# Dilated and banded attention: a step's transposes issued before its value products

## The chip, the cores and the metric

The program runs on one core of a Trainium2 chip, in one launch. Its time is the device time in microseconds, as the median of several executions. A core has five engines with a queue of instructions each: TensorE (PE, whose weight loads stand in the profile as PEld), VectorE (DVE), ScalarE (ACT), GpSimd (POOL) and SyncE (SP, which here only issues DMAs). They wait for each other by semaphores.

## The reference

Two layers of an encoder on 1024 tokens of width 1024, in float32. In each layer one input projection feeds four branches of attention: A (latent attention) and B (grouped queries) see all tokens; C is dilated, with 12 heads in three groups of dilation 1, 4 and 16 and 64 steps to either side; D is banded, 4 heads with 128 tokens to either side and a learned sink. Each branch is gated, projected and merged. What matters here is the banded core of C and D, in the reference's words:

```python
logits = jnp.einsum("bnqkgd,bnskd->bnkgqs", qb, kband).astype(jnp.float32) * scale + bias
logits = jnp.where(mask[None, :, None, None], logits, NEG_INF)
m = jnp.max(logits, axis=-1, keepdims=True)
...
    e = jnp.exp(logits - m)
    ssum = jnp.sum(e, axis=-1, keepdims=True)
p = (e / ssum).astype(v.dtype)
out = jnp.einsum("bnkgqs,bnskd->bnqkgd", p, vband).reshape(b, lp, hk, g, dv)[:, :L]
```

## The kernel before

The attention is cut into units: one head and 128 queries, against 128 to 384 keys. A layer has 32 units in A, 32 in B, 96 in C (six passes of 16 units, two for each dilation) and 32 in D. The order on every engine is written out by hand as one loop over steps, and a unit passes through several steps.

On TensorE, for C (`n == 2`) and D (`n == 3`), step `s` does the following, in this order:

- the logits of unit `s` (L1119 and L1120: two products 256 or 384 columns wide), after a wait for the maxima of unit `s-2`;
- the value products of unit `s-3` (`values`, L1145): the transposed probabilities from `ptsb`, as the stationary operand, times 64 columns of values, one product for each chunk of 128 keys. They wait until VectorE has copied the unit's transposes out of PSUM (L2130), and until the output bank is free;
- the transposes of the probabilities of unit `s-2` (`transposes`, L1130), one for each chunk, into one of two PSUM banks. They wait for the exponentials (ACT, L1530) and for the bank;
- in C, in the first two or three steps of each pass, transposes of values (`value_transposes`, L982), which wait for ScalarE's copy of the projected values (L1563);
- filler work: in C ten 512-wide products of the next pass's projection (L961; eight in the last pass; the 15th step of a pass has four and the 16th none, in the passes that have 144 products to place), in D fifteen 512-wide products of the merge of branch C (also L961). A filler that begins a PSUM bank waits until VectorE has emptied it (L1983).

Each product in plain float32 stands in the trace as two records with a weight load each: a unit of C with two chunks has four L1145 records, one with three chunks six. A transpose has one.

On VectorE a step has the biased minimum of unit `s` (L1882), in D the outputs of unit `s-3` (L1933), the copy of the transposes of unit `s-2` to `ptsb` (L2130), and now and then the rests of the next pass's operands (L1983). On ScalarE it has the exponential of unit `s` (L1530), in C the copy of the output of unit `s-3` (L1537) with a store, and the emptying of filler banks (L1563, L1569).

The numbers of the PSUM banks and the counts on the semaphores follow from a plan made ahead (`plan_units`), in the order of the transposes alone.

Of the kernel before, what the change touches and what calls it, by code (L numbers as in the profile page):

```python
# [129 lines left out]
def build(nc, x, norm_g, w_in, q_norm_g, kv_norm_g, w_q_up, w_kv_up, gqa_q_g, gqa_k_g, win_sink,  # L130
          t5_table, w_branch, w_out, final_g, c_onehot, c_mask, c_rope_a, c_rope_b, c_ident,
          out):
    with ExitStack() as ctx:
# [257 lines left out]
        def wait_tbank(eng, g, l):  # L391

            if g >= 2:
                who, n = tgroups[g - 2]
                eng.wait_ge((t_freed_dve if who == "dve" else t_freed_act)[l], n)
# [32 lines left out]
        for n in range(NB):  # L428
# [13 lines left out]
            if n == 0:  # L442
                t = []
                u0 = len(units)
# [6 lines left out]
            elif n == 1:  # L451
                t = []
                u0 = len(units)
# [7 lines left out]
            elif n == 2:  # L461
                for g, r in enumerate(STRIDES):
                    L = S // r
                    table_g = bias_mid if g == 1 else biasb
                    for hp in range(2):
                        t = [tile([(C_OFF + w * C_W + g * BW + hp * P, P, 0)]) for w in (1, 0, 2)]
                        u0 = len(units)
# [30 lines left out]
            else:  # L498
# [5 lines left out]
                u0 = len(units)  # L504
# [25 lines left out]
        def lags(u0):  # L530

            return (1, 2, 3) if units[u0]["ring"] == 2 else (2, 3, 4)
# [163 lines left out]
        def freed(l, f):  # L696

            signal, count = fill_freed_at[f]
            return signal[l], count
# [10 lines left out]
        def inc(ins, signal, n=1):  # L710

            ins.then_inc(signal, n)
# [198 lines left out]
        def _(pe):  # L911
# [5 lines left out]
            for l in range(DEPTH):  # L917
# [45 lines left out]
                def fills_part(f0, tt, m0, m1):  # L963

                    for m in range(m0, min(m1, 2 * len(tt) * FILL_MMS)):
                        j, i = divmod(m, FILL_MMS)
                        t, f = tt[j // 2], f0 + j
                        if i == 0:
                            pe.wait_ge(w_split[l], t + 1)
                            wait_fill(f)  # L970
                        ins = one_product(ps[:, fill_bank[f], :], t, j % 2, i)
                        if i == FILL_MMS - 1:
                            inc(ins, fill_ready[l])

                def value_transposes(p, v):
                    g, idx, rows = p["v_groups"][v]
                    if v == 0:

                        pe.wait_ge(*freed(l, p["fill"] + (5 if "g" in p else 7)))
                    wait_tbank(pe, g, l)  # L980
                    for i, wi in enumerate(idx):
                        ins = pe.transpose(ps[0:rows, 4 + g % 2, i * P:(i + 1) * P],  # L982
                                           window_tokens(p["windows"][wi], STRIDES[p["g"]] if "g" in p else 1),
                                           ident[:, :])
                    inc(ins, t_ready[l])

                def wait_operands(p):

                    if "g" not in p:
                        pe.wait_ge(t_freed_act[l], tgroups[p["v_groups"][-1][0]][1])  # L990
                    pe.wait_ge(*freed(l, p["fill"] + (3 if "g" in p else 5)))
                    pe.wait_ge(stack_twice[l], 4 * fill_copy[p["fill"] + 1][2])
                    if p is branches[2]["passes"][0]:
                        pe.wait_ge(*freed(l, p["fill"] + 5))
# [116 lines left out]
                def logits(s):  # L1111
                    u = units[s]
                    q_rest = u.get("q_rest")
                    if q_rest is not None:
                        pe.wait_ge(aq_set[l], s // 2 + 1)
                    for c in range(0, u["k"].shape[1], HALF):
                        w = min(HALF, u["k"].shape[1] - c)
                        dst = u["product_at"][:, c:c + w]
                        pe.matmul(dst, u["q"], u["k"][:, c:c + w], start=True, stop=False)  # L1119
                        ins = pe.matmul(dst, u["q"], u["k_rest"][:, c:c + w], start=False, stop=q_rest is None)  # L1120
                        if q_rest is not None:
                            ins = pe.matmul(dst, q_rest, u["k"][:, c:c + w], start=False, stop=True)  # L1122
                    inc(ins, lg_ready[l])

                def transposes(s):
                    pe.wait_ge(exp_done[l], s + 1)
                    for g, chunks in units[s]["groups"]:
                        wait_tbank(pe, g, l)
                        for i, (m, c0, _) in enumerate(chunks):
                            ins = pe.transpose(ps[0:m, 4 + g % 2, i * P:(i + 1) * P],  # L1130
                                               units[s]["prob"][:, c0:c0 + m], ident[:, :])
                        inc(ins, t_ready[l])

                def values(s, u0):
                    nonlocal pg
                    u = units[s]
                    if s - 2 >= u0:
                        v = units[s - 2]
                        pe.wait_ge(o_freed_dve[l] if v["who"] == "dve" else o_freed_act[l], v["o_count"])
                    n, total = 0, len(u["chunks"])  # L1140
                    for g, chunks in u["groups"]:
                        who, count = tgroups[g]
                        pe.wait_ge(t_freed_dve[l] if who == "dve" else t_freed_act[l], count)
                        for i, (m, _, v) in enumerate(chunks):
                            ins = pe.matmul(u["o"], ptsb[0:m, pg % 2, i * P:(i + 1) * P], v,  # L1145
                                            start=n == 0, stop=n == total - 1)
                            n += 1
                        pg += 1
                    inc(ins, pv_done[l])
# [83 lines left out]
                for b in branches:  # L1233
                    n = b["n"]
                    p = b["passes"][0]
                    u0, u1 = b["span"]
# [97 lines left out]
                    lt, lv, ly = lags(u0)  # L1334
                    keys_tile = branches[3]["passes"][0]["tiles"][:1]
                    if n >= 2:
                        for s in range(u0, u1 + ly):
                            k, i = divmod(s - u0, 16)
                            if s < u1:
                                if n == 2 and k and i == 0:  # L1340
                                    wait_operands(b["passes"][k])
                                if s - 2 >= u0:

                                    pe.wait_ge(nm_set[l], s - 1)
                                logits(s)
                            if n == 3 and s - lv == u0:
                                pe.wait_ge(*freed(l, b["gate_fill"] + 3))
                            if u0 <= s - lv < u1:
                                if n == 2 and (s - lv - u0) % 16 == 0:
                                    pe.wait_ge(t_freed_act[l], tgroups[b["passes"][(s - lv - u0) // 16]["v_groups"][-1][0]][1])  # L1350
                                values(s - lv, u0)
                            if u0 <= s - lt < u1:
                                transposes(s - lt)
                            if n == 2 and s < u1:
                                if i < len(b["passes"][k]["v_groups"]):
                                    value_transposes(b["passes"][k], i)
                                if k + 1 < len(b["passes"]):

                                    after = b["passes"][k + 1]
                                    fills_part(after["fill"], after["tiles"], PART * i, PART * (i + 1))  # L1360
                                else:
                                    fills_part(b["gate_fill"], b["gate_tiles"] + keys_tile, GATE_PART * i, GATE_PART * (i + 1))
                            if n == 2 and s >= u1:
                                m = GATE_PART * 16 + TAIL_PART * (s - u1)
                                fills_part(b["gate_fill"], b["gate_tiles"] + keys_tile, m, m + TAIL_PART)
                            if n == 3 and s < u1:
                                merge_part(15 * (s - u0), 15 * (s - u0 + 1))
                            if n == 3 and 0 <= s - u1 < 2:

                                pe.wait_ge(nm_set[l], u1)  # L1370
                                merge_gate_ahead(b, s - u1)
                            if n != 2 and u0 <= s - ly < u1 and units[s - ly]["head"] == HEADS - 1:
                                v = units[s - ly]
                                pe.wait_ge(o_freed_dve[l], v["o_count"])
                                y_transposes(next(y), yn[:, v["st"] % 2, :])
                        for v in units[u1 - 2:u1]:
                            pe.wait_ge(o_freed_dve[l] if v["who"] == "dve" else o_freed_act[l], v["o_count"])
# [1108 lines left out]
```

## Time and profile before

| what | value |
| --- | --- |
| median of 3 runs | 2727.71 us (2723.93 to 2729.89) |
| the profiled execution | 2725.23 us, its span 2723.4 us |
| TensorE busy | 2643.5 us, 97% of the span |
| weight loads busy | 2216.6 us, 81% |
| VectorE, ScalarE, GpSimd busy | 1286.8, 1039.8, 897.5 us |
| chain that ended last | PE 87%, DVE 5%, ACT 4% |

The profile is one execution. A line of it names the source line, the engine, the operation and the operands. A TensorE record's start is when the product was let in, and its end is modelled, so that neighbouring records overlap: lengths are best read from the start of one product to the start of a later one of the same kind. The stretches with C are 683 to 965 us and 2024 to 2305 us, those with D 1025 to 1180 us and 2365 to 2520 us.

### The profile page before, as it was taken

How to read it: one execution, taken by the hardware profiler on the slowest of the kernel's cores; microseconds unless marked ns; L12 is line 12 of the kernel's file. 1: busy time of each engine (PE TensorE's matmuls, PEld its weight loads, DVE VectorE, ACT ScalarE, POOL GpSimd, SP SyncE). 2: the span in 40 equal slices, each digit the busy share in tenths (PEclk: the TensorE clock that was granted, in tenths of full speed). 3: DMA queues.
4: the chain of work that ended last, by engine and by line, in shares of the span. 5: the costliest groups of instructions: out<-in, count | busy, mean ns of one | idle time of the engine just before them, and what ended most of it. 6: DMA issues, size and time to landing. Idle time of an engine off the chain costs nothing.

```text
span 2723.4 us, 36386 instructions
## 1 busy us (share of the span) xinstructions
PE 2643.5 (97%) x13796; PEld 2216.6 (81%) x13796; DVE 1286.8 (47%) x2697; ACT 1039.8 (38%) x2138; POOL 897.5 (33%) x634
## 2 busy tenths in 40 slices
PE   7999999999999999999999999999999999999998
PEld 5688878878888888878897878888888888888787
DVE  3575365722344365542346734575224343555223
ACT  4385115611444525521225831175024445354111
POOL 2274331033243342233423734200334342422232
PEclk9999999999999999999999999999999999999999
DMA  4200111021111231111420011100211113211122
GB/s 145 63 9 19 50 44 30 1 55 47 41 48 49 61 95 44 30 39 45 157 75 9 9 38 49 45 10 1 70 40 51 47 44 94 65 39 30 49 101 93
DMA packets 201415, 138.02 MB, mean 51 GB/s; under 512 B 20968, under 2 KB 187496, under 8 KB 201208
## 3 DMA queue, kind: packets, MB, share of 16 engines
q1 hardware_dynamic: 187420, 129.21, 16.7%
q10 hardware_dynamic: 13824, 6.49, 0.8%
q8 instruction: 112, 1.84, 0.3%
q14 instruction: 59, 0.48, 0.1%
HBM read 120.77 MB, written 19.10 MB: 51 GB/s over the span
## 4 chain that ended last, share of the span: by engine, by line
PE 87%; DVE 5%; ACT 4%; issue 2%; DMA 1%; SPq 1%; POOL 1%; ACTq 0%; POOLq 0%; DVEq 0%
PE ps L961 24%; PE ps L924 10%; PE ps L926 10%; PE ps L925 10%; PE ps L1199 5%; PE ps L1145 4%; PE ps L1164 3%; PE ps L1027 3%; PE ps L1029 3%; PE ps L1028 3%; PE ps L1119 3%; PE ps L1120 2%; PE ps L1130 2%; ACT prob L1530 1%; PE ps L1440 1%
## 5 line engine op out<-in xcount | busy, mean ns | idle before, releaser
L2356 POOL CAST wh<-wraw 128x1024 fp32r<-128x1024 f32 (+3 forms) x148 | 167.3, 1131 | 1551.1 <-PE ps L926 788.3
L924 PE MATMUL ps<-xh,wh 128*128 128x512 f32 x1088 | 426.7, 392 | 2.2 <-ACT pt_split L1756 2.2
L926 PE MATMUL ps<-xh,wl 128*128 128x512 f32 x1088 | 423.7, 389 | 0.0
L925 PE MATMUL ps<-xl,wh 128*128 128x512 f32 x1088 | 423.4, 389 | 0.0
L2358 POOL TENSOR_TENSOR wl<-wraw,wh 128x1024 fp32r<-128x1024 f32 (+3 forms) x148 | 391.5, 2646 | 11.9
L961 PE MATMUL ps<-xh,wh 128*128 128x512 f32 x896 | 366.4, 409 | 5.2 <-POOL wl L2358 2.5
L961 PE MATMUL ps<-xh,wl 128*128 128x512 f32 x896 | 357.3, 399 | 0.0
L961 PE MATMUL ps<-xl,wh 128*128 128x512 f32 x896 | 356.4, 398 | 0.0
L1585 ACT ACTIVATE gs<-ps 128x512 f32<-128x512 f32 x96 | 57.0, 598 | 518.5 <-PE ps L926 514.0
L924 PEld LDWEIGHTS ps<-xh,wh 128*128 128x128 f32 x1088 | 204.3, 188 | 44.2 <-ACT pt_split L1756 3.0
L926 PEld LDWEIGHTS ps<-xh,wl 128*128 128x128 f32 x1088 | 204.2, 188 | 43.0
L925 PEld LDWEIGHTS ps<-xl,wh 128*128 128x128 f32 x1088 | 204.4, 188 | 41.6
L2085 DVE TENSOR_TENSOR pt_slots<-ps,pt_slots 128x512 fp32r<-128x512 f32 x256 | 171.5, 685 | 83.4 <-ACT pt_slots L1674 81.6
L961 PEld LDWEIGHTS ps<-xh,wh 128*128 128x128 f32 x896 | 168.9, 188 | 39.4 <-issue 9.5
L961 PEld LDWEIGHTS ps<-xh,wl 128*128 128x128 f32 x896 | 168.6, 188 | 33.7
L961 PEld LDWEIGHTS ps<-xl,wh 128*128 128x128 f32 x896 | 169.2, 189 | 30.2 <-issue 1.0
L1530 ACT ACTIVATE prob<-prob,cst 128x192 f32<-128x192 f32 (+2 forms) x192 | 86.7, 451 | 270.3 <-DVE cst L1882 270.2
L1882 DVE CUSTOM_DVE_ANT_0 prob<-ps,biasb 128x256 f32<-128x256 f32 (+3 forms) x192 | 77.3, 402 | 224.6 <-PE ps L1120 223.4
L2004 DVE TENSOR_TENSOR gs<-ps,gs 128x512 f32<-128x512 f32 x64 | 44.2, 690 | 269.9 <-ACT gs L1585 266.6
L1674 ACT ACTIVATE pt_slots<-ps 128x512 fp32r<-128x512 f32 x256 | 148.5, 600 | 31.9 <-PE ps L1164 26.0
L1874 DVE TENSOR_REDUCE nm<-ps 128x1 f32<-128x1024 f32 x128 | 155.6, 1216 | 8.9 <-PE ps L1122 6.3
L1164 PE MATMUL ps<-ident,prob 128*128 128x128 f32 x864 | 129.2, 277 | 11.4 <-DVE pt_slots L2085 4.8
(308 smaller groups left out, 5216.7 us busy)
## 6 DMA issues: line engine op xcount, KB each, us to landing
wraw<-in_w_in_dram SPq DMA_DIRECT2D x128, 512.0 KB, 3.9
acc<-in_x_dram SPq DMA_DIRECT2D x16, 512.0 KB, 6.8
wraw<-in_w_branch_dram SPq DMA_DIRECT2D x64, 128.0 KB, 3.9
wraw<-in_w_out_dram SPq DMA_DIRECT2D x16, 512.0 KB, 3.5
dil_out<-cst ACTq DMA_DIRECT2D x96, 66.0 KB, 1.6
toep<-toep_row SPq DMA_DIRECT2D x16, 256.0 KB
xres<-acc SPq DMA_DIRECT2D x8, 512.0 KB, 2.6
acc<-xres SPq DMA_DIRECT2D x8, 512.0 KB, 7.4
```

Of the source, the lines that this page charges most:

```text
L924: pe.matmul(dst, ah, bh, start=i == 0, stop=False)
L925: pe.matmul(dst, ah, bl, start=False, stop=False)
L926: last = pe.matmul(dst, al, bh, start=False, stop=i == len(ks) - 1)
L961: return pe.matmul(dst, w, x_part, start=m == 0, stop=m == 3 * len(ks) - 1)
L1164: ins = pe.transpose(ps[0:m, 4 + g % 2, i * P:(i + 1) * P], units[s]["prob"][:, c0:c0 + m], ident[:, :])
L1199: ins = pe.matmul(u["product"], v, pair_probs((s - 3 - later) // 2, rest, j), start=j == 0 and rest == 0, stop=j == ST - 1 and rest == 1)
L1530: inc(act.activation(dst, src, ACT.Exp, bias=bias, scale=-1.0, accum_out=total), exp_done[l])
L1674: inc(act.activation(pt_slots[:, x % SLOTS, 0, 4 * part:4 * part + 4, :], ps[:, 4 + g % 2, :].rearrange("p (j t) -> p j t", t=P), ACT.Copy ...
L1874: inc(dve.tensor_reduce(dst, u["logits"], AX.X, ALU.min), nm_set[l])
L2085: inc(dve.tensor_tensor(pt_slots[:, slot, 1, some, :], ps[:, 4 + g % 2, :].rearrange("p (j t) -> p j t", t=P), pt_slots[:, slot, 0, some, ...
L2356: inc(pool.tensor_copy(high, raw), w_hi[l])
L2358: ins = pool.tensor_tensor(rest, raw, high.bitcast(F32), ALU.subtract)
```

## The change

In the step loop of TensorE for C and D, the value products of unit `s-3` are remembered and issued behind the transposes of unit `s-2`. The wait for the value groups of a pass (`t_freed_act`) stays where it was, ahead of both.

```diff
@@ -1348,9 +1348,13 @@
                             if u0 <= s - lv < u1:
                                 if n == 2 and (s - lv - u0) % 16 == 0:
                                     pe.wait_ge(t_freed_act[l], tgroups[b["passes"][(s - lv - u0) // 16]["v_groups"][-1][0]][1])
-                                values(s - lv, u0)
+                                ready_values = s - lv
+                            else:
+                                ready_values = None
                             if u0 <= s - lt < u1:
                                 transposes(s - lt)
+                            if ready_values is not None:
+                                values(ready_values, u0)
                             if n == 2 and s < u1:
                                 if i < len(b["passes"][k]["v_groups"]):
                                     value_transposes(b["passes"][k], i)
```

An ordinary step of C on TensorE, before (in these rows x2 counts instructions, not records; `yh` holds queries, `att_split` keys):

```order
L961 MATMUL ps<-xh,wl 128x512
L1119 MATMUL ps<-att_split,yh 128x256
L1120 MATMUL ps<-att_split,yh 128x256
L1145 MATMUL ps<-rows_buf,ptsb 128x64 x2
L1130 MATMUL ps<-ident,prob 128x128 x2
L961 MATMUL ps<-xh,wh 128x512
```

and now:

```order
L961 MATMUL ps<-xh,wl 128x512
L1119 MATMUL ps<-att_split,yh 128x256
L1120 MATMUL ps<-att_split,yh 128x256
L1130 MATMUL ps<-ident,prob 128x128 x2
L1145 MATMUL ps<-rows_buf,ptsb 128x64 x2
L961 MATMUL ps<-xh,wh 128x512
```

The value products now stand directly in front of a 512-wide product; before, a transpose stood between.

The last step of a pass of C and the first of the next on TensorE, before:

```order
L1119 MATMUL ps<-att_split,yh 128x256
L1120 MATMUL ps<-att_split,yh 128x256
L1145 MATMUL ps<-rows_buf,ptsb 128x64 x2
L1130 MATMUL ps<-ident,prob 128x128 x2
L1119 MATMUL ps<-bk_stack,yl 128x256
L1120 MATMUL ps<-bk_stack,yl 128x256
L1145 MATMUL ps<-rows_buf,ptsb 128x64 x2
L1130 MATMUL ps<-ident,prob 128x128 x2
L982 MATMUL ps<-ident,prob 128x128 x4
L961 MATMUL ps<-xh,wh 128x512
```

and now:

```order
L1119 MATMUL ps<-att_split,yh 128x256
L1120 MATMUL ps<-att_split,yh 128x256
L1130 MATMUL ps<-ident,prob 128x128 x2
L1145 MATMUL ps<-rows_buf,ptsb 128x64 x2
L1119 MATMUL ps<-bk_stack,yl 128x256
L1120 MATMUL ps<-bk_stack,yl 128x256
L1130 MATMUL ps<-ident,prob 128x128 x2
L1145 MATMUL ps<-rows_buf,ptsb 128x64 x2
L982 MATMUL ps<-ident,prob 128x128 x4
L961 MATMUL ps<-xh,wh 128x512
```

Here the value products of the first step still have a transpose behind them (L982), and those of the last step now a 256-wide product. In D the same exchange is made with three chunks:

```order
L1120 MATMUL ps<-bk_stack,att_split 128x384
L1130 MATMUL ps<-ident,prob 128x128 x3
L1145 MATMUL ps<-rows_buf,ptsb 128x64 x3
L961 MATMUL ps<-xh,wh 128x512
L961 MATMUL ps<-xl,wh 128x512
```

Counted over the whole order of now, 232 groups of L1145 have a product that is no transpose behind them (218 an L961, 10 an L1119, 4 an L924); before, 2 had. The other engines run the same instructions in the same order as before.

## Rows read from the trace of the kernel before

**Rows 1.** Busy time in the two stretches of C and of D.

```profile
core 0: us, PE busy (x) PEld busy (x) DVE busy (x) ACT busy (x) POOL busy (x), PEclk, DMA share, GB/s
683.00:965.00 282.00, 278.66 (x1585) 238.94 (x1586) 113.01 (x344) 132.31 (x366) 101.88 (x76) 1.00 0.20 51
1025.00:1180.00 155.00, 154.68 (x839) 133.18 (x838) 88.56 (x259) 79.93 (x147) 37.88 (x18) 1.00 0.13 35
```

**Rows 2.** TensorE's waits in the first C, 683 to 965 us.

```profile
PE ps L1145 <- DVE ptsb L2130: 2.1, 5, 0.4
PE ps L961 <- DVE yl L1983: 0.6, 1, 0.6
PE ps L982 <- ACT prob L1563: 0.2, 1, 0.2
```

**Rows 3.** Timeline of TensorE: an ordinary step of C.

```profile
692.55 0.28 PE L1120 MATMUL ps<-att_split,yh 128*128 128x256 f32 x1
692.67 0.56 PE L1145 MATMUL ps<-rows_buf,ptsb 128*128 128x64 f32 x4
693.06 0.39 PE L1130 MATMUL ps<-ident,prob 128*128 128x128 f32 x2
693.21 0.48 PE L961 MATMUL ps<-xh,wh 128*128 128x512 f32 x1
693.52 0.40 PE L961 MATMUL ps<-xl,wh 128*128 128x512 f32 x1
```

**Rows 4.** Timeline of TensorE: end of C, value products with and without a transpose behind.

```profile
962.83 0.39 PE L961 MATMUL ps<-xh,wl 128*128 128x512 f32 x1
963.06 0.33 PE L1145 MATMUL ps<-att,ptsb 128*128 128x64 f32 x2
963.22 0.28 PE L1130 MATMUL ps<-ident,prob 128*128 128x128 f32 x1
963.26 0.48 PE L961 MATMUL ps<-xh,wh 128*128 128x512 f32 x1
963.57 0.40 PE L961 MATMUL ps<-xl,wh 128*128 128x512 f32 x1
...
964.04 0.39 PE L961 MATMUL ps<-xh,wh 128*128 128x512 f32 x1
964.27 0.33 PE L1145 MATMUL ps<-att,ptsb 128*128 128x64 f32 x2
964.40 0.48 PE L961 MATMUL ps<-xl,wh 128*128 128x512 f32 x1
964.72 0.40 PE L961 MATMUL ps<-xh,wl 128*128 128x512 f32 x1
```

**Rows 5.** Timeline of TensorE in A: four 64-wide records behind two transposes.

```profile
540.00 0.38 PE L1219 MATMUL ps<-ident,rows_buf 128*128 128x128 f32 x2
540.21 0.56 PE L1187 MATMUL ps<-fold,ptsb 128*128 128x64 f32 x4
540.61 0.61 PE L1164 MATMUL ps<-ident,prob 128*128 128x128 f32 x4
```

**Rows 6.** Timeline of TensorE in A: four 64-wide records ahead of 512-wide products.

```profile
553.92 0.55 PE L1187 MATMUL ps<-fold,ptsb 128*128 128x64 f32 x4
554.28 0.48 PE L924 MATMUL ps<-xh,wh 128*128 128x512 f32 x1
554.60 0.39 PE L925 MATMUL ps<-xl,wh 128*128 128x512 f32 x1
554.83 0.40 PE L926 MATMUL ps<-xh,wl 128*128 128x512 f32 x1
```

**Rows 7.** Timeline of TensorE, last and first step of two passes of C.

```profile
729.25 0.28 PE L1120 MATMUL ps<-att_split,yh 128*128 128x256 f32 x1
729.36 0.55 PE L1145 MATMUL ps<-rows_buf,ptsb 128*128 128x64 f32 x4
729.75 0.39 PE L1130 MATMUL ps<-ident,prob 128*128 128x128 f32 x2
...
730.10 0.28 PE L1120 MATMUL ps<-bk_stack,yl 128*128 128x256 f32 x1
730.82 0.63 PE L1145 MATMUL ps<-rows_buf,ptsb 128*128 128x64 f32 x4 [0.44 <-DVE ptsb L2130]
731.28 0.39 PE L1130 MATMUL ps<-ident,prob 128*128 128x128 f32 x2
731.51 0.60 PE L982 MATMUL ps<-ident,prob 128*128 128x128 f32 x4
```

**Rows 8.** Timeline of VectorE in the same steps.

```profile
729.64 0.29 DVE L1882 CUSTOM_DVE_ANT_0 prob<-ps,biasb 128x192 f32<-128x192 f32 x1
730.25 0.42 DVE L2130 COPY ptsb<-ps 128x256 f32<-128x256 f32 x1 [0.31 <-PE ps L1130]
```

**Rows 9.** Timeline of ScalarE in the same steps.

```profile
728.19 0.46 ACT L1530 ACTIVATE prob<-prob,cst 128x192 f32<-128x192 f32 x1 [2.40 <-DVE cst L1882]
728.55 0.19 ACT L1530 ACTIVATION_READ_ACCUMULATOR prob<-prob,cst 128x1 f32 x1
730.53 0.58 ACT L1563 ACTIVATE prob<-ps 128x512 f32<-128x512 f32 x1
```

**Rows 10.** Timeline of TensorE: a filler product that waits for its bank.

```profile
762.38 0.40 PE L961 MATMUL ps<-xh,wl 128*128 128x512 f32 x1
762.83 0.47 PE L961 MATMUL ps<-xh,wh 128*128 128x512 f32 x1
```

## The prediction

> **What bounds the kernel now.** I read the busy time by stretch first, then TensorE's waits, then the timeline of single steps. In the stretches of C and D TensorE is busy for 278.66 of 282 us and 154.68 of 155 us, at full granted clock (1.00), and no other engine is over half busy there [rows 1] but for VectorE and ScalarE in D, at 57% and 52%. So the reader is to see that in these loops nothing is late except TensorE itself: every nanosecond that its order costs is added to the span, and the most that a better cover of waits can bring is what TensorE waits. That is 2.1 us for the copy of the transposes, in 5 waits of a layer [rows 2], 4 us in both layers.
>
> **What the change takes away.** The value products wait for the copy (L2130) only where the filler work is missing, at the turn of a pass: L1145 starts at 730.82, 0.15 behind the end of the copy at 730.67, where TensorE could have had it at 730.10 + 0.12 = 730.22 [rows 7, 8]. With the transposes first, both ends of this wait move. The copied transposes are issued 0.39 earlier in the step before (at 729.36 and not 729.75 [rows 7]); the copy then follows the minimum that ends at 729.93 and ends near 730.40 [rows 8]. The value products come behind two transposes, at 730.22 + 0.22 = 730.44, and wait until 730.40 + 0.15 = 730.55. The wait is nearly gone. What is late next is the transposes of values, L982: they need ScalarE's L1563, which ends at 731.11 [rows 9], and with the same 0.15 they cannot start before 731.26. They start at 731.51 now [rows 7]. So a turn gains 0.25 us, not 0.6. There are five turns in a layer; at the fifth L982 already waits for L1563 [rows 2], and there the gain is nothing. The term is 8 x 0.24 = 1.9 us.
>
> **What it adds.** No instruction is added, but the neighbours change. Read how long a group of 64-wide records takes by what stands behind it. Behind a product comes the group, then a transpose: four records take 693.06 - 692.67 = 0.39 [rows 3] and 540.61 - 540.21 = 0.40 [rows 5], two take 0.16 [rows 4]. With a 512-wide product behind, the start of that product is recorded early (0.03 behind a transpose, and the product after it 0.31 later, where two 512-wide ones stand 0.23 apart), so I read to the second one: four records take 554.60 - 553.92 - 0.23 = 0.45 [rows 6]. For two records, from a 512-wide product to the second one behind the group: 964.72 - 964.04 = 0.68 without a transpose, 963.57 - 962.83 = 0.74 with one [rows 4]. A transpose takes 0.11 (0.21 for two in rows 5), so it should have added 0.11 and adds 0.06. Both readings say the same: a 64-wide record that has a transpose behind it is 0.05 us shorter than one with anything else behind it, each other one being 0.11. The transposes themselves cost the same with either neighbour: two of them ahead of a 64-wide record take 0.21 [rows 5].
>
> Before, every group of value products had a transpose behind it, in all but 2 cases. Now 232 have an L961, L1119 or L924, which makes 230 more (84 steps in each C, the 95 with both parts less the 11 in which L982 follows; 31 steps in each D). An ordinary step goes from 0.97 (692.55 to 693.52 [rows 3]) to 1.02. Start times are rounded to 0.01, so the price lies between 0.04 and 0.06; I take 0.047, and 230 x 0.047 = 10.8 us. The bounds are 230 x 0.06 = 13.8 above, and nothing below, if 512-wide weights can be got ready behind a 64-wide record in this place, which no row shows.
>
> The Trainium skill (TensorE: Matmul & The Clock Gate, LDWEIGHTS) gives a load as P/1.2, by which an estimate for 128 columns is 107 ns, and its section "Step-by-step: what each phase is for" says that TensorE pulls the next load ahead of running products. By the second rule alone the order would be free and the sum would be the gain of 1.9 us; the records against it are those of rows 4 and 6, and the first rule fits the 0.11 of each record.
>
> **What of it is hidden.** In four of the six passes of a layer (the second to the fifth) one filler waits for its bank: it comes at 762.83 and not at 762.61 [rows 10], and after an idle 0.6 in the fifth pass [rows 2]. That wait ends by a chain through ScalarE and VectorE which starts at the logits of the step before, and two groups of value products lie between. It is at least 0.2 long, so it swallows 2 x 0.047 each time: I count 8 of them, 0.8 us. The last step of a pass ends in the wait for L1563, which swallows its 0.047 ten times: 0.5 us.
>
> **Costed at nothing.** The transposes are issued 0.39 earlier (0.61 in D) relative to their exponentials; at 731.28 the exponential of that unit had ended at 728.74 [rows 7, 9], and a step takes over 1.7 us even where it has no filler. The bank that they wait for was read by a copy one step before. The value products end 0.2 to 0.3 later in the step; ScalarE's copy of the output stands behind an exponential that ends later still, and in D VectorE has idle time. SP, POOL and the DMAs see no change.
>
> **The sum.** 10.8 - 1.9 - 0.8 - 0.5 = +7.6 us. Against the profiled execution's own 2725.2 us that is 2732.8; it lies 2.5 us below the median of the runs, so against the median of 2727.7 I forecast 2735.3, rounded to 2735 us, slower by 0.28%.
>
> **The rivals.**
>
> 1. Faster: the load is hidden after all. Then the wait at the turns is all that changes. For it speaks the wait that is there; against it that the price was read in two places of different width and agrees. Its time is 2727.7 - 1.9 = 2725.8, down to 2723.6 if L982 had not to wait and the whole 4.1 us went. It decides at the first L961 behind the value products: with a pitch of 0.97 for the step and not 1.02 it is this one. Chance 0.13.
> 2. Partly paid: the price is as read, but the waits swallow more of it, since a slower TensorE meets banks that are already free, or some groups pay less than those of rows 4 and 6. With 120 to 150 of the 230 groups paying, 5.6 to 7 less 3.2: 2730 to 2732, within 0.2%. Against it: outside the turns and 8 bank waits no wait stands in these stretches [rows 1, 2]. Chance 0.14.
> 3. Slower than that: a price also between transposes and 64-wide records, which rows 5 show to be absent at one place only, or 0.06 and not 0.047, with no gain at the turns: 13.8 to 16, so 2741 to 2744. Chance 0.07.
> 4. The change does nothing, because the transposes wait for exponentials in every step and the order is made good: nearly excluded, since the exponential has 2.5 us in hand at a turn, where steps are shortest [rows 7, 9]. 2728, chance 0.02.
>
> **How the numbers follow.** The forecast has 0.64, with its own range 2731 to 2739: the price from 0.04 to 0.06 gives +5.9 to +10.5, and the median moves by 1 or 2 us on its own. For 8 in 10 I add rival 2 and part of rival 1: 2726 to 2740. What a measurement of this kernel can tell from no change is 0.2%, 5.5 us: slower begins at 2733.2. The forecast's own range lies mostly above it (0.54 of its 0.64), rival 3 wholly: slower 0.61. Same: 0.10 of the forecast, rivals 2 and 4 and most of rival 1: 0.34. Faster: 0.05.
>
> **What would show it.** In the changed kernel an ordinary step of C should go from L1120 to the second L961 in 1.02 us instead of 0.97, and its whole pitch from 3.17 to 3.22; a step of D should grow by 0.05 as well. The idle time of L1145 for L2130 should fall from 4.1 us to under 1, and L982 should wait for L1563 at every turn. The stretches of C should grow by about 2.7 us each and those of D by 1.5 each; wider groups of value products should not cost more than narrow ones. The prediction is wrong if the step keeps its 0.97, or if the stretches grow while the step does not.

## The result, and the profile after

Against the kernel before, run on the same chips, the changed one takes 2732.25 us in the median of 15 runs (2730.29 to 2736.33) where the one before takes 2725.44 us: a ratio of 1.0025, 95% interval 1.0018 to 1.0032. It is 6.8 us slower, a quarter of a per cent, and the interval does not reach 1. The forecast was 7.6 us slower, 2735 us, with its own range from 2731 to 2739. The profiled execution of the changed kernel has a span of 2730.2 us, also 6.8 more than before.

The busy times of the same two stretches, which now begin and end a little later (columns as in [rows 1]):

```profile
683.00:968.00 285.00, 282.82 (x1587) 243.51 (x1588) 107.53 (x344) 132.93 (x367) 102.36 (x76) 1.00 0.19 50
1028.00:1184.00 156.00, 155.68 (x837) 133.43 (x836) 88.58 (x259) 79.92 (x147) 37.85 (x18) 1.00 0.13 35
```

TensorE is as full as it was, and the same number of products takes longer. VectorE is busy 5.5 us less in C with as many instructions, because its copies of the transposes now find their data and overlap the end of the minimum ahead of them; the idle time in front of the copies of two chunks was 17.0 us in C before and is 0.3:

```profile
L2134 DVE COPY ptsb<-ps 128x256 f32<-128x256 f32 x64 | 27.0, 422 | 0.3 <-PE ps L1145 0.3
```

That is a great deal of waiting taken from an engine that is not the bottleneck, and it is worth nothing but the turns. The ordinary step of C on TensorE's timeline, the one of [rows 3], and the start of the next step:

```profile
692.86 0.28 PE L1119 MATMUL ps<-att_split,yh 128*128 128x256 f32 x1
692.97 0.28 PE L1120 MATMUL ps<-att_split,yh 128*128 128x256 f32 x1
693.09 0.38 PE L1130 MATMUL ps<-ident,prob 128*128 128x128 f32 x2
693.31 0.56 PE L1145 MATMUL ps<-rows_buf,ptsb 128*128 128x64 f32 x4
693.68 0.48 PE L961 MATMUL ps<-xh,wh 128*128 128x512 f32 x1
693.99 0.40 PE L961 MATMUL ps<-xl,wh 128*128 128x512 f32 x1
...
696.07 0.28 PE L1119 MATMUL ps<-gs_split,yh 128*128 128x256 f32 x1
```

From L1120 to the second L961 it is 693.99 - 692.97 = 1.02 us, where [rows 3] have 0.97. The pitch, from the L1119 of one step to the L1119 of the next, is 3.21 us (696.07 - 692.86). The four value records and the first filler take 0.68 (693.31 to 693.99), less 0.23 for the filler: 0.45, as the four of [rows 6].

The turn of a pass, which answers to [rows 7], with ScalarE's copy of the values ([rows 9]):

```profile
730.15 0.28 PE L1120 MATMUL ps<-att_split,yh 128*128 128x256 f32 x1
730.27 0.38 PE L1130 MATMUL ps<-ident,prob 128*128 128x128 f32 x2
730.49 0.56 PE L1145 MATMUL ps<-rows_buf,ptsb 128*128 128x64 f32 x4
...
731.06 0.28 PE L1120 MATMUL ps<-bk_stack,yl 128*128 128x256 f32 x1
731.17 0.38 PE L1130 MATMUL ps<-ident,prob 128*128 128x128 f32 x2
731.39 0.57 PE L1145 MATMUL ps<-rows_buf,ptsb 128*128 128x64 f32 x4
732.08 0.66 PE L982 MATMUL ps<-ident,prob 128*128 128x128 f32 x4
```

```profile
731.44 0.59 ACT L1567 ACTIVATE prob<-ps 128x512 f32<-128x512 f32 x1
```

The value products no longer wait for the copy of the transposes. L982 does wait: it starts at 732.08, right behind the end of ScalarE's L1567 at 732.03. From the L1120 of the last step to L982 it is 1.93 us, where [rows 7] have 2.26. TensorE's waits in C say the same, against [rows 2]: L1145 has gone from the list, and L982 has 0.4 instead of 0.2. That one wait of L982 is at the fifth turn. At the other four the list names none, since the modelled ends of the value products reach over the idle time; there the starts show it, with 1.92 or 1.93 us from the L1120 of the last step to L982 at each of the eight turns of both layers. The 0.8 us of L1119 is no news: it stands ahead of the first logits of C, and the kernel before has it too, though [rows 2] do not list it (the row by itself, which is of before).

```profile
PE ps L1119 <- ACT prob L1567: 0.8, 1, 0.8
PE ps L961 <- DVE yl L1987: 0.5, 1, 0.5
PE ps L982 <- ACT prob L1567: 0.4, 1, 0.4
```

```profile
PE ps L1119 <- ACT prob L1563: 0.8, 1, 0.8
```

To compare the stretches of all kernels I take the start of the first and the last logits of a stretch (L1119; C begins with `gs_split` and ends with `bk_stack`, D is `bk_stack,att_split`). For the changed kernel, where the columns after the count are the duration in ns (least, median, most) and the first and last start:

```profile
L1119 PE MATMUL ps<-bk_stack,yl x48: 277/278/366, 730.9 to 961.9; 128*128 128x256 f32 x48
L1119 PE MATMUL ps<-gs_split,yh x24: 277/278/366, 683.7 to 921.8; 128*128 128x256 f32 x24
L1119 PE MATMUL ps<-bk_stack,att_split x32: 277/333/421, 1028.5 to 1173.7; 128*128 128x384 f32 x24, 128*128 128x256 f32 x8
```

The last column is the median distance from one L1119 to the next, over the steps of C with two chunks and ten fillers.

| kernel (profiled execution) | first C, us | first D, us | ordinary step of C, us |
| --- | --- | --- | --- |
| before | 276.2 | 144.0 | 3.17 |
| changed | 278.2 | 145.2 | 3.21 |
| transposes on both sides (e1) | 275.4 | 144.0 | 3.17 |
| new order at the turns alone (e2) | 275.1 | 144.0 | 3.17 |
| one by one in turn (e5) | 272.6 | 141.8 | 3.11 |
| the same, transpose first at the turns (e6) | 272.1 | 141.8 | 3.11 |
| order before, 128 columns of values (e3) | 279.3 | 145.3 | 3.20 |
| order now, 128 columns of values (e4) | 278.4 | 145.1 | 3.21 |
| order before, plain products for transposes (e7, one run) | 296.2 | 154.3 | 3.44 |

The changed kernel's growth sits in these stretches: 2.0 and 2.2 us in the two C, 1.3 in each D (from the unrounded starts), 6.8 in all. What lies outside them differs by less than 0.1 us in sum, though parts of it differ by up to 1.0 (see the last section).

### The profile page after: what moved, and what is told of

It reads as the page before. It is cut to its first block, busy times and chain, and to the rows that moved or that the text cites. A ratio compares the mean times of both kernels' runs of the same rounds, so it can differ in the third digit from the quotient of the medians.

```text
span 2730.2 us, 36382 instructions
## 1 busy us (share of the span) xinstructions
PE 2652.1 (97%) x13796; PEld 2225.1 (81%) x13796; DVE 1276.0 (47%) x2697; ACT 1039.6 (38%) x2138; POOL 897.0 (33%) x634
## 4 chain that ended last, share of the span: by engine, by line
PE 87%; DVE 5%; ACT 4%; issue 2%; DMA 1%; SPq 1%; POOL 1%; ACTq 0%; POOLq 0%; DVEq 0%
PE ps L961 24%; PE ps L924 10%; PE ps L926 10%; PE ps L925 10%; PE ps L1199 5%; PE ps L1145 3%; PE ps L1164 3%; PE ps L1027 3%; PE ps L1029 3%; PE ps L1028 3%; PE ps L1119 3%; PE ps L1120 2%; PE ps L1130 2%; ACT prob L1534 1%; PE ps L1444 1%
## 5 line engine op out<-in xcount | busy, mean ns | idle before, releaser
L924 PE MATMUL ps<-xh,wh 128*128 128x512 f32 x1088 | 426.6, 392 | 2.2 <-ACT pt_split L1760 2.2
L961 PE MATMUL ps<-xh,wh 128*128 128x512 f32 x896 | 366.1, 409 | 5.2 <-POOL wl L2362 2.7
L961 PE MATMUL ps<-xh,wl 128*128 128x512 f32 x896 | 357.1, 399 | 0.0
L961 PE MATMUL ps<-xl,wh 128*128 128x512 f32 x896 | 356.5, 398 | 0.0
L924 PEld LDWEIGHTS ps<-xh,wh 128*128 128x128 f32 x1088 | 204.3, 188 | 44.4 <-ACT pt_split L1760 3.0
L961 PEld LDWEIGHTS ps<-xh,wh 128*128 128x128 f32 x896 | 169.0, 189 | 39.3 <-issue 9.4
L961 PEld LDWEIGHTS ps<-xh,wl 128*128 128x128 f32 x896 | 168.7, 188 | 33.4
L961 PEld LDWEIGHTS ps<-xl,wh 128*128 128x128 f32 x896 | 169.1, 189 | 30.3 <-issue 1.0
```

The source lines that it names most:

```text
L924: pe.matmul(dst, ah, bh, start=i == 0, stop=False)
L961: return pe.matmul(dst, w, x_part, start=m == 0, stop=m == 3 * len(ks) - 1)
```

## The experiments

**e1: the value products between the transposes.** In the step, all transposes but the last go ahead, the last one behind.

```diff
-                                values(s - lv, u0)
-                            if u0 <= s - lt < u1:
-                                transposes(s - lt)
+                                both = u0 <= s - lt < u1
+                                if both:
+                                    mixed(s - lv, s - lt, u0, lambda nv, nt: "t" * (nt - 1) + "v" * nv + "t")
+                                else:
+                                    values(s - lv, u0)
+                            elif u0 <= s - lt < u1:
+                                transposes(s - lt)
```

`mixed` issues the same products with the same waits, in the order of the letters. On record before it ran:

> The value products stand between the transposes: all transposes of the step but the last ahead of them, the last one behind. Theory N (what costs is the neighbour behind the last value product: 0.05 us whenever it is no transpose): an ordinary step of C keeps the pitch of before, 3.17 us, the stretches of C and D keep their 280.9 and 161.0 us, and the time is that of before to within 2 us. Rival F (the step pays because transposes now stand directly behind the logits, or because value products stand behind a transpose): the pitch is 3.21 as in the changed kernel and the time is 5 to 7 us over before.

Measured: ratio to before 0.9989 (0.9980 to 0.9997); C 275.4, D 144.0. A step on TensorE's timeline:

```profile
700.79 0.28 PE L1120 MATMUL ps<-gs_split,yh 128*128 128x256 f32 x1
700.91 0.28 PE L1177 MATMUL ps<-ident,prob 128*128 128x128 f32 x1
701.02 0.56 PE L1167 MATMUL ps<-rows_buf,ptsb 128*128 128x64 f32 x4
701.41 0.28 PE L1177 MATMUL ps<-ident,prob 128*128 128x128 f32 x1
701.45 0.48 PE L961 MATMUL ps<-xh,wh 128*128 128x512 f32 x1
701.76 0.40 PE L961 MATMUL ps<-xl,wh 128*128 128x512 f32 x1
```

A transpose stands directly behind the logits and value products directly behind a transpose, as in the changed kernel, and yet L1120 to the second L961 is 0.97, and the pitch stays at 3.17. D is as before to 0.1 us. (The 280.9 and 161.0 us of the expectation are from another way to count a stretch than the table's; what was to be tested is that the stretches keep their length.) Rival F falls; what counts is what stands behind the last value product. The time came out 3 us under before, where I had allowed 2: each C is 0.8 shorter, since at the turns the value products come behind a transpose and wait 1.3 us in all and not 2.1; the rest of the 3 us is outside C and D, where the edit changes nothing.

**e2: the new order at the turns alone.**

```diff
+                                turn = n == 2 and s < u1 and (k and i == 0 or i == 15 and k + 1 < len(b["passes"]))
+                                if turn:
+                                    transposes(s - lt)
                                 values(s - lv, u0)
-                            if u0 <= s - lt < u1:
+                            else:
+                                turn = False
+                            if u0 <= s - lt < u1 and not turn:
```

> The new order only in the last step of a pass of C and in the first step of the next one (10 turns, so 20 steps of 254); everywhere else the order of before. Theory N with the turn as I worked it out: 10 groups pay 0.047, which falls into a wait, and 8 turns gain 0.25 us: 2 us under before, too little for the comparison, but the stretches of C shrink by 1.0 us each and those of D not at all. Rival W (a wait saved at a turn is given back within the pass, by the next wait for a bank): stretches of C as before to within 0.3 us.

Measured: 0.9993 (0.9984 to 1.0002), not to be told from no change; C 275.1, so 1.1 shorter, and D 144.0, the same. The gain at the turns shows in the stretches, not in the medians. It is kept to the end of the stretch and has the size of the forecast, 1.0 us. Rival W falls.

**e5: value products and transposes one by one in turn.** The order is `"".join("v" * (i < nv) + "t" * (i < nt) for i in range(4))` in the call above.

> Value products and transposes one by one in turn: value, transpose, value, transpose. Counted over the order, 488 of 496 value products have a transpose behind them, where before 254 had one and in the changed kernel 24. Theory N: 234 more short ones than before, 0.047 each: 11 us under before, 0.4%; an ordinary step of C has a pitch of 3.13 instead of 3.17, a step of D is 0.09 shorter. Rival L (the last record of the whole group is short only because the load of the transposes starts while several products of one bank are in flight, so it is one saving a step): no change from before. Rival F (each change between the two kinds costs): slower than before by 234 x 2 x 0.02, some 10 us.

Measured: 0.9961 (0.9949 to 0.9974), 11 us under before. A step:

```profile
701.73 0.28 PE L1120 MATMUL ps<-att_split,yh 128*128 128x256 f32 x1
701.85 0.33 PE L1167 MATMUL ps<-rows_buf,ptsb 128*128 128x64 f32 x2
702.02 0.28 PE L1177 MATMUL ps<-ident,prob 128*128 128x128 f32 x1
702.14 0.33 PE L1167 MATMUL ps<-rows_buf,ptsb 128*128 128x64 f32 x2
702.31 0.28 PE L1177 MATMUL ps<-ident,prob 128*128 128x128 f32 x1
702.34 0.48 PE L961 MATMUL ps<-xh,wl 128*128 128x512 f32 x1
702.66 0.39 PE L961 MATMUL ps<-xh,wh 128*128 128x512 f32 x1
```

Now both value products of the unit have a transpose behind them, and L1120 to the second L961 is 0.93. The saving comes once for each pair of a value product and a transpose behind it, so it is no matter of the group. It is 11 us for 234 more such pairs, 0.047 each. That is a mean: the pitch in C fell by 0.06 to 3.11 where 3.13 was expected, of which 0.05 is between L1120 and the second L961 (0.973 to 0.924 in the median) and the rest among the fillers, and D fell by 2.2 us, which is 0.04 for each of its pairs. Why the two differ stays open. Rivals L and F fall.

**e6: as e5, with the transpose first in each pair at the turns** (the condition of e2).

> The last one with the transpose first in the last step of a pass of C and the first step of the next. Theory N with the turn: 1 to 2 us under the kernel that alternates everywhere, all of it in the stretches of C (some 0.2 us a turn, in four turns of five). Rival W: the same as that kernel.

Measured: 0.9952 (0.9940 to 0.9965), 2710.91 us in the median on a chip where before takes 2725.78. C is 0.5 shorter than in e5 and D the same, so some 1 us for both layers, the lower end of what was expected. This version beats both kernels: by 0.5% the one before, and so, by the two ratios, by some 0.7% the changed one, which it was not run against.

**e3 and e4: value products of 128 columns, in the order of before and of now.** Each takes the values of two heads; half of the result is not used. The edit shown is that of the dilated units with two chunks; those with one chunk and the units of D are widened in the same way, and the product writes `u["wide"]`.

```diff
-                                    chunks = [(P, x, cv[hp][:, place[(c, first + x)], cols]) for x in (0, P)]
+                                    chunks = [(P, x, cv[hp][:, place[(c, first + x)], :]) for x in (0, P)]
...
-            u["o"] = ps[:, 6 + s % 2, 0:HD]
+            u["wide"] = ps[:, 6 + s % 2, 0:2 * HD]
+            mine = more["e"] if "e" in more else more["head"] // 2
+            u["o"] = ps[:, 6 + s % 2, mine * HD:(mine + 1) * HD]
```

> The order of before, but each value product of C and D takes 128 columns of values (those of two heads, of which one is used) instead of 64, so its pass through the array takes as long as a transpose's. Theory E (a 64-wide record is done in about 0.06 us and then stands waiting for the next weights, which take 0.11; in front of a transpose they are there sooner): with 128 columns each record fills its 0.11, the saving in front of a transpose is gone, and doubling the values costs just that: 254 x 0.047 = 12 us less what waits swallow, so the stretches of C grow by 2.2 to 3 us each, those of D by 1.4, as in the changed kernel, and the step of C has a pitch of 3.21. Rival M (a change of mode: whatever stands in front of a transpose is cheap): records stay 0.05 short in front of a transpose, C and D as before, 3.17. Rival R (the width counts in full, as for 512-wide ones): each of the 992 records costs 0.05 more, 45 us in all.

> The changed kernel's order with the same 128 columns of values. Theory E: nothing but the 24 products that still have a transpose behind them can grow: the time of the changed kernel plus at most 1 us, a pitch of 3.21 in C, and the same time as the wide kernel in the order of before to within the gain at the turns (2 us). Rival M: as the changed kernel too, but then 10 us over the wide kernel in the order of before. Rival R: 45 us over the changed kernel.

Measured: e3 1.0036 (1.0022 to 1.0051), e4 1.0032 (1.0019 to 1.0045). The step of e3, in the order of before:

```profile
701.31 0.28 PE L1122 MATMUL ps<-gs_split,yh 128*128 128x256 f32 x1
701.43 0.61 PE L1147 MATMUL ps<-rows_buf,ptsb 128*128 128x128 f32 x4
701.88 0.38 PE L1132 MATMUL ps<-ident,prob 128*128 128x128 f32 x2
702.01 0.48 PE L963 MATMUL ps<-xh,wh 128*128 128x512 f32 x1
702.33 0.39 PE L963 MATMUL ps<-xl,wh 128*128 128x512 f32 x1
```

Four records ahead of a transpose take 0.45 where the 64-wide ones took 0.39 [rows 3], L1120 to the second L963 is 1.02, and the pitch is 3.20. D is as long as in the changed kernel, C longer by about the gain at the turns that only the new order has; its 3.1 us over before are a little more than the 2.2 to 3 expected. In the changed kernel's order the doubled width costs nothing in the stretches: C 278.4 against 278.2, D 145.1 against 145.2. (The ratio of e4 is 0.0007, 1.9 us, above that of the changed kernel; the two intervals overlap, and the stretches show none of it.) Rivals M and R fall. It fits theory E, that of a 64-wide record's 0.11 about half is idle unless a transpose stands behind it; the idle half itself no row shows.

**e7: plain products with the identity in place of the transposes,** in the order of before.

```diff
-                            ins = pe.transpose(ps[0:m, 4 + g % 2, i * P:(i + 1) * P],
-                                               units[s]["prob"][:, c0:c0 + m], ident[:, :])
+                            ins = pe.matmul(ps[0:m, 4 + g % 2, i * P:(i + 1) * P],
+                                            units[s]["prob"][:, c0:c0 + m], ident[:, :], start=True, stop=True)
```

> The order of before, with the transposes of probabilities in C and D made by plain float32 products with the identity instead of transposes, so each has two records. One look at the step. If the short last record belongs to a transpose behind it, the value products are now 0.05 longer (0.44 to 0.45 for four records in front of them, and a step of C of 3.17 + 0.22 + 0.05 = 3.44 us). If it belongs to any float32 product with the identity as moving operand, or to 128 columns behind 64, they stay 0.39 and the step is 3.39.

Measured (one run, 2788.52 us):

```profile
712.22 0.28 PE L1119 MATMUL ps<-gs_split,yh 128*128 128x256 f32 x1
712.34 0.28 PE L1120 MATMUL ps<-gs_split,yh 128*128 128x256 f32 x1
712.46 0.56 PE L1145 MATMUL ps<-rows_buf,ptsb 128*128 128x64 f32 x4
712.85 0.66 PE L1130 MATMUL ps<-ident,prob 128*128 128x128 f32 x4
715.66 0.28 PE L1119 MATMUL ps<-att_split,yh 128*128 128x256 f32 x1
```

The two readings that I put together came apart. The pitch is 3.44, which says that the saving has gone: two more records at 0.11 make 0.22, and there is 0.05 on top. But the value group still takes 0.39 from its start to the next group's start, where 0.44 to 0.45 was expected. The 0.05 stands in the group behind. I go by the pitch, since the loop pays that: the saving belongs to a transpose behind the value product, not to the identity or to 128 columns. By the pitch alone the 0.05 could also be a cost of the plain products themselves; the weight loads under "The cause" speak against that. It also shows that a distance of starts between two kinds of record is not their cost.

## Why the prediction was right

**The price.** The step was forecast to go from 0.97 to 1.02 and did; D's step with three chunks was to grow by 0.05, and D grew by 1.3 us over 144 (1.29 unrounded), which is 31 steps of 0.042. The pitch in C came to 3.21, not 3.22; the fillers behind the group make up for a little of the price. So the mechanism was right and the price over the whole loop was 0.042, at the low end of the 0.04 to 0.06 that the prediction gave: 9.7 us for 230 groups, not 10.8. e5 has 0.047 in the mean, with the opposite sign. The price was read from starts of different kinds of record [rows 3, 5]; e7 shows that this reading can mislead. What held it up were the readings from one 512-wide product to another [rows 4].

**The turn.** A gain of 0.25 was forecast. From the last step's L1120 to L982 the time fell by 0.33, but the first L982 record is then longer; to the first filler behind, by 0.28. At the other turns that was 0.23 to 0.25, and at the fifth nothing, as said: 2.0 us in all, where the sum has 1.9. The successor wait was named rightly: L982 for ScalarE's copy. The value products were to keep a wait of 0.11 there and have none, since the copy starts before the minimum ahead of it has ended and is done 1.03 us behind the L1120 of the last step, where the prediction had 1.15; as L982 ends the turn, that slip cost the forecast nothing.

**What is swallowed.** The wait for a bank answers to [rows 10] in these rows of the changed kernel:

```profile
763.26 0.40 PE L961 MATMUL ps<-xh,wl 128*128 128x512 f32 x1
763.67 0.47 PE L961 MATMUL ps<-xh,wh 128*128 128x512 f32 x1
```

It is 0.41 instead of 0.45. So it swallowed 0.04 and not the 0.09 of the forecast. The other three of the first C swallowed 0.08, 0.05 and 0.07; in the second C two swallowed 0.03 and 0.07, one nothing, and one wait grew by 0.04. That makes 0.3 us where the sum has 0.8. The prediction treated each such wait as one that takes in all of a delay, and they took in less than half.

**The sum.** It gave +7.6, of which 2.3 in each C and 1.5 in each D. The stretches from the first logits to the last grew by 2.0 and 2.2 us and by 1.3 each. With the terms as measured it is 9.7 - 2.0 - 0.3 - 0.5 = 6.9 (the last term not measured by itself), against the 6.8 of the stretches. Two slips partly cancel: the price was 1.1 us too high and what is swallowed 0.5 too high; that the total came so near owes something to luck. Of the 3 us between 2735 and the measured 2732.25, 2.3 are the median of before, taken from three runs. In its last part the prediction put the growth of C at 2.7, which does not follow from its own sum; the sum was right and that figure was not.

**The rivals.** That the load is hidden (1) is excluded by the step and, with a cause, by e3 and e4. That only part of the groups pays (2) is excluded by the pitch of every common kind of step: in C 3.17 became 3.21, 2.37 became 2.42, 2.82 became 2.88 and 1.79 became 1.83; in D 4.87 became 4.92, and 4.75 and 4.73 became 4.78. That transposes cost something ahead of value products (3) is excluded by e1. That the exponentials hold up the transposes (4) did not happen: no L1130 stands among the waits.

**The cause.** Shown: a value product of 64 columns is shorter by 0.05 when a transpose stands behind it (e1, e5), and not when it is itself 128 columns wide (e3); e7 says the same of a plain product of the same operands in the transpose's place, by its pitch. That fits a load of 0.11 us for the next weights which a record of 0.06 cannot cover, and a load for a transpose which takes about half of that.

The trace has the weight loads as records of their own (PEld), and they bear this out. These are the loads of the transposes in the first C (ns: least, median, most) in the changed kernel, e5 and e7, and last the value products' in the changed kernel:

```profile
L1130 PEld LDWEIGHTS ps<-ident,prob x160: 137/142/144, 689.9 to 965.3; 128*128 128x128 f32 x160
L1177 PEld LDWEIGHTS ps<-ident,prob x158: 192/194/200, 695.7 to 962.6; 128*128 128x128 f32 x158
L1130 PEld LDWEIGHTS ps<-ident,prob x302: 188/192/192, 691.8 to 964.7; 128*128 128x128 f32 x151
L1145 PEld LDWEIGHTS ps<-rows_buf,ptsb x160: 186/192/193, 693.2 to 930.7; 128*128 128x128 f32 x160
```

Where there is nothing to save (now, and in e3 with a median of 141), the load of a transpose is recorded with 142 ns and that of a plain product with 192, so 0.05 less; with plain products in their place (e7) the 192 is back. In e5, where every transpose stands behind a 64-wide value product, its load is recorded with 194: it starts some 0.06 us behind the load before it, where the loads of plain products start 0.11 apart, so it begins the saved 0.05 sooner. As far as the recorded ends can be trusted, the loads of transposes are shorter by the size of the price. What remains argued is that the load alone makes the saving: no run changes the length of a load and nothing else. The Trainium skill (TensorE: Matmul & The Clock Gate, LDWEIGHTS) has loads at P/1.2, an estimate of 107 ns for 128 columns. That agrees with the 0.11 at which plain records follow each other, but not with the 192 ns that such a load is recorded with, nor with what stands in front of a transpose.

## What to carry to other kernels

Where TensorE is full, the order of its products has a price of its own. Here a product of 64 columns did not cover the load of the weights behind it: a transpose behind it saved 0.05 us, and widening it to 128 columns was free where no transpose followed. When an edit swaps two groups, look at all the neighbours that change, find each pair somewhere else in the trace, and multiply by the count: a gain of 0.25 us at 8 turns was outweighed by some 0.04 us at 230 steps. Read prices from one record to the next of the same kind, around the whole group.

## What the runs showed that I had not expected

The alternating order, which only turned the finding round, is worth 11 us, and 15 with the turns (12.5 of them in the stretches of C and D), more than the change under study.

Part of the spread between executions lies outside C and D, and the traces show two sources of it. One is the granted clock. Two neighbouring stretches of the second layer in the kernel before (columns as in [rows 1]):

```profile
1772.00:1775.30 3.30, 1.66 (x7) 0.71 (x5) 2.91 (x3) 2.68 (x4) 3.22 (x2) 1.00 0.00 0
1775.30:1778.70 3.40, 3.36 (x12) 2.87 (x13) 1.32 (x3) 1.69 (x3) 0.64 (x1) 0.50 0.48 109
```

In the second of them the clock lay at the lower of its two levels (1.2 and 2.4 GHz); in the first, still at the upper one, TensorE had been busy for half the time. In the changed kernel, which comes to the same place about 3 us later and pauses there too (busy for 2.31 of the 3.40 us from 1775.3), it stayed at the upper level. From the last logits of the first D to the first of the second C it is 854.1 us before and 853.1 in the changed kernel, a difference that belongs to no edit: e3, in the order of before, has the same fall of the clock and 854.2, and e4, in the new order, has none and 853.1. The other is the transfer of the dilated outputs behind the first C, for which VectorE waits; this is before, and in e2 it is 1.6:

```profile
DVE ptsb L2166 <- DMA att<-dil_out: 3.6, 1, 3.6
```

With the longer wait TensorE waits 1.0 us in turn, and the way from the first C to the first D is 1.1 us longer. Both values turn up with either order: before has 3.6 in the first layer and 1.6 in the second, the changed kernel 3.5 and 1.6. So a profiled span alone tells nothing under some 2 us, while within one execution the first and second C agree to 0.3 us and the two D to 0.1.
